# Rope key as an fp32 product on column halves, latent splits on VectorE, a reordered opening, and prompt scores moved behind the last local turning, in a two-layer streaming encoder step

## The reference, cut to what matters

```python
h = rmsnorm(x, lp['norm_mix'])
proj = h @ lp['w_in']
u_pool, q_b, k_b, v_b, q_lat, kv_lat, kr_raw, gates = jnp.split(proj, IN_SPLITS, axis=-1)
...                                   # A: trailing mean pooling; B: windowed attention
cq = rmsnorm(q_lat, lp['mla_q_norm'])
qm = (cq @ lp['mla_w_qup']).reshape(B, T, MLA_HEADS, MLA_QK_DIM)     # then rope, norm
c_kv = rmsnorm(kv_lat, lp['mla_kv_norm'])
k_rope = apply_rope(kr_raw, pos)
km, vm = mla_expand(c_kv, k_rope, lp['mla_w_kvup'], lp['mla_qk_k_norm'])
ym = softmax(qm km / sqrt(96), chunk-causal) vm                      # C: latent attention
x = x + (sum_i sigmoid(gate_i(h)) * (branch_i @ w_branch_i)) @ w_out
x = x + SwiGLU(rmsnorm(x, lp['norm_ffn']))
```

## Time and profile before

| | us |
|---|---|
| median of 3 executions (lowest, highest) | 1072.66 (1070.98, 1074.01) |
| the profiled execution, and its span | 1072.71, 1070.9 |
| TensorE busy in the span | 1056.9 |
| VectorE, ScalarE, GpSimd busy | 632.9, 507.0, 312.7 |
| mean granted clock of TensorE, as a share of full speed | 0.997 |

### The profile page before, as it was taken

One profiled execution on the slowest core, in us unless ns is written; L12 is line 12 of the kernel. 1 busy time (PEld: TensorE's weight loads), 2 busy tenths in 40 slices (PEclk: granted clock), 3 DMA queues, 4 the chain that ended last, 5 costly groups with the idle time before them and its releaser, 6 DMA issues.

```text
span 1070.9 us, 19944 instructions
## 1 busy us (share of the span) xinstructions
PE 1056.9 (99%) x7558; PEld 1020.8 (95%) x7558; DVE 632.9 (59%) x1047; ACT 507.0 (47%) x895; POOL 312.7 (29%) x230
## 2 busy tenths in 40 slices
PE   8899999999999999999999999999999999999998
PEld 6889988999999999999989999889999999999998
DVE  5659655445666665643566795544457666556444
ACT  6455745444454434334454466444445443443332
POOL 1655454651121111100124645565312111110000
PEclk9999999999999999999999999999999999999999
DMA  6446333324444444445413444332345354444443
GB/s 229 117 119 180 125 117 101 110 92 152 142 136 159 159 153 151 143 162 168 158 65 135 137 131 125 118 101 96 121 146 167 115 168 151 156 139 155 158 142 123
DMA packets 48769, 147.90 MB, mean 138 GB/s; under 512 B 8480, under 2 KB 13952, under 8 KB 48704
## 3 DMA queue, kind: packets, MB, share of 16 engines
q1 hardware_dynamic: 41552, 142.79, 41.5%
q10 hardware_dynamic: 7152, 4.20, 1.3%
HBM read 143.75 MB, written 3.22 MB: 137 GB/s over the span
## 4 chain that ended last, share of the span: by engine, by line
PE 93%; DVE 4%; ACT 1%; POOL 1%; issue 0%; ACTq 0%; POOLq 0%; DVEq 0%
PE psum L479 28%; PE psum L480 27%; PE psum L481 27%; PE psum L642 1%; PE psum L603 1%; PE psum L634 1%; PE psum L626 1%; PE psum L567 1%; POOL ssum L1731 1%; PE psum L570 1%; PE psum L568 1%; PE psum L587 1%; PE psum L588 1%; PE psum L674 0%; PE psum L590 0%; PE psum L846 0%
## 5 line engine op out<-in xcount | busy, mean ns | idle before, releaser
L479 PE MATMUL psum<-AH,WH 128*128 128x320 f32 x1344 | 421.1, 313 | 1.2 <-DVE krt L1537 0.7
L481 PE MATMUL psum<-AH,WL 128*128 128x320 f32 x1344 | 415.3, 309 | 0.0
L480 PE MATMUL psum<-AL,WH 128*128 128x320 f32 x1344 | 415.2, 309 | 0.0
L479 PEld LDWEIGHTS psum<-AH,WH 128*128 128x128 f32 x1344 | 252.3, 188 | 6.5 <-issue 4.2
L480 PEld LDWEIGHTS psum<-AL,WH 128*128 128x128 f32 x1344 | 252.4, 188 | 0.9
L481 PEld LDWEIGHTS psum<-AH,WL 128*128 128x128 f32 x1344 | 252.3, 188 | 0.0
L922 ACT CAST WH<-raw 128x1024 fp32r<-128x1024 f32 x175 | 182.6, 1046 | 138.5 <-PE psum L481 136.8
L1736 POOL TENSOR_TENSOR WL<-raw,WH 128x1024 fp32r<-128x1024 f32 x71 | 174.0, 2461 | 167.1 <-ACT WH L922 167.1
L1305 DVE TENSOR_TENSOR WL<-raw,WH 128x1024 fp32r<-128x1024 f32 x102 | 126.3, 1239 | 116.9 <-ACT WH L922 116.7
L1490 DVE TENSOR_TENSOR WL<-raw,WH 128x1024 fp32r<-128x1024 f32 x88 | 107.6, 1223 | 49.6 <-ACT WH L1073 48.2
L1741 POOL TENSOR_TENSOR fab<-fa,fb 128x320 f32<-128x320 f32 x44 | 38.7, 879 | 270.1 <-DVE fb L1495 270.1
(11 more groups left out here) (239 smaller groups left out, 1556.7 us busy)
## 6 DMA issues: line engine op xcount, KB each, us to landing
raw<-w_all SPq DMA_DIRECT2D x267, 512.0 KB, 3.5
y_out<-X SPq DMA_DIRECT2D x8, 160.0 KB, 3.0
ckv<-lat_in ACTq DMA_DIRECT2D x2, 384.0 KB, 5.4
X<-x_in ACTq DMA_DIRECT2D x2, 320.0 KB, 8.5
X<-x_in ACTq DMA_DIRECT2D x1, 640.0 KB, 10.4
lat_out<-ckv ACTq DMA_DIRECT2D x2, 320.0 KB, 4.3
scratch<-brel SPq DMA_DIRECT2D x8, 63.8 KB, 4.1
bias<-scratch SPq DMA_DIRECT2D x8, 48.0 KB, 4.2
```

Of the source, the lines that this page charges most:

```text
L479: mm(out, WH[:, slot, c0:c0 + cols], high, start=first, stop=False)
L480: mm(out, WH[:, slot, c0:c0 + cols], low, start=False, stop=False)
L481: return mm(out, WL[:, slot, c0:c0 + cols], high, start=False, stop=last)
```

## The change

- The rope tile becomes 8 fp32 products of 64 columns from unsplit weights and unsplit x. VectorE multiplies the 64 weight columns by the norm's gain into `WF`, in the place of the unit's `WH`. Even chunks add up in partitions 0 to 63, odd ones in 64 to 127. ScalarE copies one half to SBUF (`rope_half`) and VectorE adds the other. `rstd` is then applied in a step of its own.
- VectorE makes the low parts of units 6, 7 and 8, which GpSimd made. In layer 0 GpSimd makes that of unit 2 at the very start.
- `key_rows` and `value_rows` of the first block wait for the low weights only before their last two products.
- The first weight unit comes in two transfers, one by each queue. The table load stands between ScalarE's transfers. The norm work of layer 0 starts earlier and in another order. Seven warm-up products run instead of four.
- The prompt scores of item 5 go behind the turning of item 4, before its values. The sample scores stay where they were.
- In layer 0 the kv latent's sum of squares is in the middle of the second query tile.

```diff
-WARM = 4
+WARM = 7
@@ SP
-        sp.dma_start(raw[:, 0, :], w_all[stored(0)]).then_inc(raw_ready[0], 16)
+        sp.dma_start(raw[:, 0, 0:512], w_all[stored(0)][:, 0:512]).then_inc(raw_ready[0], 16)
@@ TensorE
+        def rope_columns(l):
+            open_tile(l, T_KR)
+            pe.wait_ge(s.split_ready, l * NU + U_KR + 1)
+            for k in range(KC):
+                half = slice(k % 2 * 64, k % 2 * 64 + 64)
+                last = mm(psum[half, tbank(T_KR), 0:T], WF[:, k, :], X[:, k, :], start=k < 2, stop=k >= KC - 2)
+            last.then_inc(s.tile_full, 1)
@@ key_rows (value_rows alike)
-                pe.wait_ge(s.split_ready, l * NU + U_KVK + 1)
+                pe.wait_ge(s.high_ready, l * NU + U_KVK + 1)
...
+            if kb == 0:
+                pe.wait_ge(s.split_ready, l * NU + U_KVK + 1)
             for c in range(2):
                 last = mm(out, ckvH[:, c, keys], wl[:, c], start=False, stop=c == 1)
@@ scores
             if i == SW_ITEMS:
-                prompt()
+                if part == 0:
+                    prompt()
+                    return
                 pe.wait_ge(s.tile_free, l * NT + item_tile(SW_ITEMS - 1) + 1)
                 last = sample()
@@ order of the tiles
-            dense(l, U_KR, T_KR)
+            rope_columns(l)
             if l == 0:
                 stat_mix(l, 0)
...
+            dense(l, U_QL, T_QL)
+            if l > 0:
+                latent_sum(l)
+            dense(l, U_QL + 1, T_QL + 1, between=(lambda: latent_sum(l)) if l == 0 else None)
@@ attention
                 turn(l, i)
-                if i + 1 < SW_ITEMS:
-                    scores(l, i + 1)
+                scores(l, i + 1)
                 values(l, i)
             for j in range(4):
                 i = SW_ITEMS + j
-                scores(l, i)
+                scores(l, i, part=1)
@@ ScalarE, opening
-        cached_latent(0)
+        cached_first(0)
+        act.wait_ge(s.warm_zero, 1)
+        A(small[:, 31:32], ssum[:, 0:1], ACT.Sqrt)
+        cached_rest(0)
         act.dma_start(X[:, 0:2, :], x_in[:, 0:2, :]).then_inc(s.x_in[0], 16)
...
+        act.wait_ge(s.half_in, 16)
         high(0, U_KVK)
         high(0, U_KVV)
         cached_high(0, 1)
+        high(0, U_KV)
...
                 key_square(l, kb)
+                if l == 0 and kb == 0:
+                    act.wait_ge(s.par_in, 16)
+                    act.wait_ge(s.x_in[0], 16)
+                    norm_chunk(l, 0, 0, square=False)
+                    norm_chunk(l, 0, 1, square=False)
                 value_copy(l, kb)
@@ VectorE
             key_columns(l, CACHED - 1)
-            low(l, U_KR)
+            dve.wait_ge(raw_ready[U_KR % RING], (l * (NU // RING) + U_KR // RING + 1) * 16)
+            TT(WF[:], raw[:, U_KR % RING, :].rearrange("p (k c) -> p k c", k=KC)[:, :, 0:64],
+               col(C_MIX, l, n=KC)[:, :, None].to_broadcast([128, KC, 64]), ALU.mult).then_inc(s.split_ready, 1)
             low(l, U_QL)
+            low(l, U_QL + 1)
             stream_rstd(l, 0)
             scaled(l, T_KV, kvr[:, 0, :])
             scaled(l, T_KV + 1, kvr[:, 1, :])
+            low(l, U_QL + 2)
...
-            TT(krt[64:128, 0, :], p[64:128, 0:T], rstd[64:128], ALU.mult).then_inc(s.tile_free, 1)
+            dve.wait_ge(s.kr_half, l + 1)
+            TT(krt[64:128, 0, :], p[64:128, 0:T], krt[64:128, 1, :], ALU.add).then_inc(s.tile_free, 1)
             dve.wait_ge(s.tile_free, l * NT + T_KR + 1)
+            link(l, TT(krt[64:128, 0, :], krt[64:128, 0, :], rstd[64:128], ALU.mult))
...
             TT(ckvL[:, :, 0:T], ckv[:, :, 0:T], ckvH[:, :, 0:T].bitcast(F32), ALU.subtract).then_inc(s.ckv_ready, 1)
+            low(l, U_POOL)
             scaled(l, T_QL + 2, qlr[:, 2, :])
@@ GpSimd
+            if l == 0:
+                pool.wait_ge(s.split_ready, U_KV)
+                low(l, U_KV)
             for kb in range(CACHED):
                 rope_keys(l, kb)
...
-            for u in range(U_QL + 1, U_POOL + 2):
-                low(l, u)
+            low(l, U_POOL + 1)
```

## The result

The changed kernel takes 1067.09 us (median of 5, 1066.81 to 1067.42); the kernel before, run beside it, takes 1073.24 (median of 5, 1070.98 to 1075.61). The ratio is 0.995, with a 95% interval of 0.9938 to 0.9962: faster by about 6 us. The forecast was 1065.9 with a range of 1062.9 to 1069.9. The profiled execution has a span of 1065.3 us against 1070.9, so 5.6 us must be found in the trace where the forecast had 6.8.

What follows compares the result with a forecast made beforehand. TensorE, busy for 1056.9 of 1070.9 us, was taken to bound the kernel. Layer 0 gains 6.0 us, layer 1 gains 1.2, scores lose 0.4, together 6.8: 1072.7 - 6.8 = 1065.9 us, range 1062.9 to 1069.9.

Steps and rivals of the forecast that it cites:

- opening, up to the kv tiles: Layer 0: first key block at about 7.3 us instead of 8.65, but first turning of keys gains only 0.25 us.
- second kv tile: Layer 0: unit 3 is split by 24.3 us, so the 0.69 us gap before this tile goes, 0.65 gained.
- rope tile with the stop behind it, layer 0: Rope-key tile takes 2.3 us instead of 3.52, 1.2 gained; TensorE's short stop before the sum-of-squares product closes, 0.4 gained.
- second query tile: Layer 0 latent stage: VectorE makes the split of GpSimd's 2.40 us that delays this tile, 0.8 us gained.
- turning of rope rows, wait of the prompt keys: Layer 0: 0.2 us gained at the turning; wait before prompt keys 1.15 instead of 2.78 us, 1.6 gained.
- clock after it, less the wait of the value rows: Layer 0 behind the prompt keys: full clock gains 1.25 us in the key and value block; value rows lose 0.35.
- layer 1: Latent stage of layer 1: TensorE has no gap there, so only the rope tile's 1.2 us can be gained.
- scores, both layers: Last local attention item: wait for `PTs` is filled, but sample scores wait for `yAL`; 0.2 us lost in each layer.
- 256 KB of the first weight unit now stand ahead of both on ScalarE's queue: Opening, layer 0: rest of the latent and X land 1.0 us later, from 0.7 at 390 GB/s or 1.3 at half.
- a first turning after 17 us: Opening, layer 0: sign that would make the prediction wrong; first turning of keys was expected near 16 us.
- rival (a): Opening: late X or issues waiting for the table; first turning 1.3 us later, perhaps slow clock 1.3 us; 1068.8; chance 0.12.
- Rival (c): Layer 0's latent wait keeps slow clock and length, VectorE's added steps taking what the port gives back; 1068.8; chance 0.08.

## Why the prediction came out as it did

| term | expected, us | measured, us |
|---|---|---|
| opening, up to the kv tiles | +0.25 | -1.6 |
| second kv tile | +0.65 | +0.7 |
| rope tile with the stop behind it, layer 0 | +1.6 | +1.5 |
| second query tile | +0.8 | +0.85 |
| turning of rope rows, wait of the prompt keys | +1.8 | +1.95 |
| clock after it, less the wait of the value rows | +0.9 | +1.25 |
| layer 1 | +1.2 | +1.0 |
| scores, both layers | -0.4 | -0.05 |
| sum | +6.8 | +5.6 |

**Right.** Direction and size: 1067.1 for 1065.9, inside the range. Five of the eight terms are within 0.2 us of their forecast. The rope tile took 2.31 us for the forecast of 2.3, and the experiment with one half confirms the reason taken from the earlier trace rows. The gap of the second kv tile closed. The `ckv` products came down to 0.55, the key wait to 0.82 us (1.15 forecast), and no slow clock followed. Layer 1 gained only in its rope tile, and 1.0 us instead of 1.2: the change from the sum's product to the first rope load takes 0.77 us where it took 0.41, with 0.44 us of idle weight load in it. The scores only moved a wait, as said; the prompt scores behind the turning cost less than 0.05 us a layer, not 0.2.

**Wrong: the opening,** in the step "256 KB of the first weight unit now stand ahead of both on ScalarE's queue ... I take 1.0: latent 9.5, X 11.6". They landed at 12.05 and 13.1. The prediction had said that "a first turning after 17 us" would make it wrong; it came at 17.99 us, so by its own sign this part is wrong. The loss of 1.6 us also lies outside the bounds given for it (1.2 gained to 1.3 lost), and the total is in range because the range was wide enough for one such miss, which is luck as far as this part goes. The first key block, too, came at 8.93 and not near 7.3. The lower bound of that part had a late table load in mind, which costs nothing, and no late latent. The sum of rival (a) had the right sign for this place (1.3 us later, for 1.8 measured) and the wrong causes: neither the table nor a slow clock, nor X, which came late but was not waited for. The step took 195 to 390 GB/s for the queue. From 5 to 8 us the changed kernel's trace shows this by queue (packets, MB, share of the 16 engines):

```profile
q1 hardware_dynamic: 437, 0.66, 65.6%
q10 hardware_dynamic: 238, 0.39, 35.4%
```

ScalarE's queue, the smaller one, moved 0.39 MB in 3 us: 130 GB/s and a third of the engines' time, not a half or all of it. At that rate 256 KB are 2.0 us. The rate is not fixed: in the same stretch the queue moved 0.50 MB in the kernel before and 0.53 MB in the experiment with one transfer. The issue came 0.5 us later as well, since the added transfer takes 0.61 us to issue; the remaining 1.0 of the 3.5 us is not split further. Then the second mistake: no schedule was made with a latent that late, in which all of ScalarE's chain hangs on it. The forecast had X as the last to come.

**Right sum, wrong reason in part.** Rival (c) speaks of the 1.6 us of the key wait as "what the port gives back": GpSimd gone from beside VectorE. The trace shows the `ckv` product 1.0 us shorter. But with GpSimd's splits put back into the changed kernel the keys start within 0.2 us of the same time. The port's gain pays for the splits that VectorE took over, and no more. From the sum's product to the prompt keys it was 16.43 us and is 13.62. Of these 2.8 us, 1.0 is the shorter `ckv` product and 1.8 lie ahead of it, at the second reciprocal. The kernel before, and then the changed kernel:

```profile
46.48 1.24 PE L781 MATMUL psum<-SQ,cst 128*128 128x320 f32 x4
...
48.31 2.15 DVE L1336 RECIPROCAL stdk<-stdk 128x320 f32<-128x320 f32 x1 [1.15 <-ACT stdk L963]
```

```profile
43.27 1.24 PE L512 MATMUL psum<-SQ,cst 128*128 128x320 f32 x4
...
45.91 2.14 DVE L1379 RECIPROCAL stdk<-stdk 128x320 f32<-128x320 f32 x1
```

The kv latent's sum of squares came behind the second query tile, and VectorE stood idle 1.73 and 1.15 us in front of the reciprocal that needs it. Now it comes in the middle of that tile, 3.2 us earlier, of which 1.4 are the tile's earlier start, and VectorE goes into the reciprocal without a wait, in spite of its added work. The forecast's schedule runs the reciprocal straight behind `scaled` and so has this in it, but gives the edit no value of its own. With GpSimd's splits put back the reciprocal starts at 44.89, as soon as ScalarE's root is done (44.87), so there the date of this sum decides. No run moved the sum back behind the tile, so its share is read from the timelines and not shown by an experiment.

The second query tile had a wait of 0.97 us on the weight-load side, for GpSimd's 2.4 us split of unit 6, which in the earlier trace rows started at 40.33 behind ScalarE's cast. That cast came at 39.15, behind ScalarE's root; the change moves it ahead of the root (an edit that the list of edits leaves out), and it comes at 33.31. With GpSimd's splits put back, the split starts at 35.23, and the second query tile has no wait before it either. Without the earlier cast VectorE would have been no help: it was in the first reciprocal until 41.43. So the 0.85 us of the second query tile belong to the earlier cast. The forecast read a cast that came late as a split that was slow.

**A slip in the range.** Its lower end counts the opening's 1.2 us whole, where 0.25 of them are in the sum already; by its own terms it should be about 1063.2, not 1062.9. Nothing hangs on it.

**The warm-ups.** The forecast gave the slow stretch of the opening no value of its own, and that was right: removing the three products brings 1.2 GHz back and costs nothing that can be told from the spread of the landings. At the prompt keys the same kind of stretch is on the path: the key and value block lasted 3.99 us at 1.2 GHz and lasts 2.74 at 2.4.

**The splits against the sums of squares** around 30 us: two of them take 3.70 us in the changed kernel where two alone take 2.44 (1.22 each). The 1.3 us named in the forecast are there, ahead of VectorE's idle stretch, and cost nothing. The same additions also stretch the `AL` steps (3.18 us for four), and that became a cost of 0.5 us in the experiments that brought the opening forward.

## What to carry to other kernels

An extra transfer on a queue costs what stands behind it there, at the rate that this queue gets while the others are busy. Read that rate from the trace by queue, take a range for it (130 to 177 GB/s in three kernels here), and redo the schedule of whoever waits for the last of these transfers. When work moves from one engine to another to end a conflict, add its own time on the new engine first: here the two cancelled. Before an experiment is read, check that its base still has the wait that the edit is meant to remove; one here had none. And where an engine seems to deliver late, look at who releases it before giving its work away.

## What the runs showed of the hardware beyond that

- Eight fp32 products of 64 output columns and 320 columns of data take 4.45 us in one column half and 2.31 us alternating between the halves.
- A VectorE instruction of 0.49 us can take 2.38 us beside a GpSimd split of 2.41: it lasts until 0.33 us after that one's end. The first `ckv` product of before does the same (52.05 against 51.70, 0.35 us). A step on only 128x3 elements, 0.17 us by itself, took 1.20 and 1.22 us and ended 0.02 us after GpSimd's split.
- After a wait of 3.4 us on the weight-load side in the middle of the kernel (squares behind the casts) TensorE's granted clock was 0.50 from 38 to 40 us, and the tile stretch took 1.4 us longer; after the 2.78 us before the prompt keys of the kernel before it was 0.50 as well, and after 0.82 us in the changed kernel 1.00.
- The seven warm-up products, 14 records, last 7.03 us in the changed kernel, 0.50 a record, where the same 128x320 form takes 0.27 a record in the earlier trace rows. The granted clock is shown as 1.00 in each of these microseconds. So in the first 8 us of this execution the record of the clock doesn't tell how fast TensorE ran; the time per record does.
